# Values of six heads in one token-major product with the forget logits as 6 more columns, values of the other heads two pairs ahead

## What is computed

```python
proj = rms_norm(x, g_pre_mix) @ w_in
mq, mk, mv, fq, fk, fv, f_logit, cvb, cvc, cvh = split(proj)   # 6 x 384, 6, 3 x 256 columns
moba = softmax(causal(mq @ mk.T / 8 + relative_bias)) @ mv     # 6 "local" heads of 64
log_f = log_sigmoid(f_logit + b_f)                             # one logit per head and token
fox = softmax(causal(fq @ fk.T / 8 + cumsum(log_f) differences)) @ fv   # 6 forgetting heads
conv = cvb * causal_conv3(cvc * cvh)
x = x + rms_norm(concat(moba, fox, conv) @ w_out, g_post_mix)
h2 = rms_norm(x, g_pre_ffn)
out = x + rms_norm((silu(h2 @ w_gate) * (h2 @ w_up)) @ w_down, g_post_ffn)
```

## Time and profile before

| what | us |
|---|---|
| median of 3 runs | 581.09 |
| the three runs | 580.45, 581.09, 581.23 |
| the profiled execution's own time | 581.22 |
| its span, first to last instruction | 579.5 |
| TensorE busy in the span | 569.5 |
| values of pair 0 and forget logits on PE | 26.04 to 35.29 |
| the loop's pairs 0 to 4 | 35.29 to about 156 |
| pair 5 | about 156 to 196.8 |

### The profile page before, as it was taken

One profiled execution on the slowest core, in us unless ns is written; L12 is line 12 of the kernel. 1 busy time (PEld: TensorE's weight loads), 2 busy tenths in 40 slices (PEclk: granted clock), 3 DMA queues, 4 the chain that ended last, 5 costly groups with the idle time before them and its releaser, 6 DMA issues.

```text
span 579.5 us, 9678 instructions
## 1 busy us (share of the span) xinstructions
PE 569.5 (98%) x3381; PEld 501.4 (87%) x3381; DVE 472.3 (82%) x788; ACT 322.6 (56%) x540; POOL 113.3 (20%) x128
## 2 busy tenths in 40 slices
PE   6999999999999999999999999999999999999996
PEld 5878888888888888899999999999999988888884
DVE  3868897988849874799888988988898788888797
ACT  6735666666645553656464645455454565547752
POOL 1111011122200010000423233242423013344100
PEclk9999999999999999999999999999999999999999
DMA  7554343333223381312232323132321459999833
GB/s 298 164 152 122 109 110 110 110 96 124 73 74 109 110 312 52 103 44 74 83 136 78 140 72 145 72 113 104 112 105 72 145 167 283 262 212 207 160 145 145
DMA packets 27322, 76.82 MB, mean 133 GB/s; under 512 B 3194, under 2 KB 3194, under 8 KB 27292
## 3 DMA queue, kind: packets, MB, share of 16 engines
q1 hardware_dynamic: 18204, 54.83, 27.0%
q0 software_dynamic: 9088, 21.61, 17.1%
HBM read 69.06 MB, written 4.22 MB: 126 GB/s over the span
## 4 chain that ended last, share of the span: by engine, by line
PE 97%; DMA 1%; ACT 1%; DVE 0%; issue 0%; SPq 0%; DVEq 0%; ACTq 0%
PE bank L1532 11%; PE bank L1534 11%; PE bank L1533 11%; PE bank L1787 8%; PE bank L1786 8%; PE bank L1785 8%; PE bank L1793 6%; PE bank L1851 6%; PE bank L1853 6%; PE bank L1855 6%; PE bank L1796 3%; PE bank L1666 3%; PE bank L1654 2%; PE bank L1578 2%; PE bank L1644 1%; PE bank L1642 1%
## 5 line engine op out<-in xcount | busy, mean ns | idle before, releaser
L1786 PE MATMUL bank<-tok_lo,form_hi 128*128 128x256 f32 x320 | 90.6, 283 | 0.0
L1787 PE MATMUL bank<-tok_hi,form_lo 128*128 128x256 f32 x320 | 90.6, 283 | 0.0
L1785 PE MATMUL bank<-tok_hi,form_hi 128*128 128x256 f32 x320 | 90.5, 283 | 0.0
L1532 PE MATMUL bank<-hn,w_hi 128*128 128x512 f32 (+1 forms) x208 | 79.8, 384 | 0.1
L1534 PE MATMUL bank<-hn,w_lo 128*128 128x512 f32 (+1 forms) x208 | 78.1, 376 | 0.0
L1533 PE MATMUL bank<-hn,w_hi 128*128 128x512 f32 (+1 forms) x208 | 77.8, 374 | 0.0
L1785 PEld LDWEIGHTS bank<-tok_hi,form_hi 128*128 128x128 f32 x320 | 60.9, 190 | 1.9
L1787 PEld LDWEIGHTS bank<-tok_hi,form_lo 128*128 128x128 f32 x320 | 61.1, 191 | 0.0
L1786 PEld LDWEIGHTS bank<-tok_lo,form_hi 128*128 128x128 f32 x320 | 61.0, 191 | 0.0
L1851 PE MATMUL bank<-dw_hi,da_hi 128*128 128x512 f32 x154 | 60.0, 389 | 0.0
L1855 PE MATMUL bank<-dw_hi,da_lo 128*128 128x512 f32 x154 | 59.9, 389 | 0.0
(11 more groups left out here) (201 smaller groups left out, 1394.5 us busy)
## 6 DMA issues: line engine op xcount, KB each, us to landing
raw<-in_w_in_units SPq DMA_DIRECT2D x24, 512.0 KB, 3.4
raw<-in_w_gate_units SPq DMA_DIRECT2D x22, 512.0 KB, 3.3
raw<-in_w_up_units SPq DMA_DIRECT2D x22, 512.0 KB, 4.2
down_x<-in_w_down POOLq DMA_DIRECT2D x15, 512.0 KB, 11.5
down_y<-in_w_down SPq DMA_DIRECT2D x10, 512.0 KB, 11.1
raw<-in_w_out SPq DMA_DIRECT2D x8, 512.0 KB, 3.3
q_lh<-q_hl POOLq DMA_DIRECT2D x12, 256.0 KB, 2.8
down_x<-in_w_down SPq DMA_DIRECT2D x5, 512.0 KB, 4.3
```

The costliest lines, as they stand in the source:

```text
L1532: nc.tensor.matmul(out_ap, sh, mh, start=first, stop=False)
L1785: nc.tensor.matmul(out_ap, sh, mh, start=first and k == 0, stop=False, skip_group_check=True)
L1786: nc.tensor.matmul(out_ap, sh, ml, start=False, stop=False, skip_group_check=True)
L1787: mm = nc.tensor.matmul(out_ap, sl, mh, start=False, stop=k == HK - 1, skip_group_check=True)
```

## The change

**Values of the local heads.** Units 2, 3 and 4 are now the value columns of pairs 0, 1 and 2. They are split, not into slots of the ring, but side by side into two new buffers `wv_hi` and `wv_lo` of 8 x 390 columns; the 6 forget columns stand behind them, as columns 384 to 389. The product is turned round: a tile of 128 tokens is the stationary operand, the 390 columns are the moving one. Four token tiles (groups 2 to 5) take 24 matmuls of 390 columns each, all before the loop. The result is token-major, so these three pairs need neither `vT` nor transposes: ACT and DVE write high and low parts straight into `v_moba`, and DVE copies the 6 logits of each tile to `f_tok`. The first two tiles run high parts first and low parts behind them.

**Forget logits.** Their own group is gone, and the buffer with its memset on POOL. In step 1 of the loop PE transposes `f_tok` in four matmuls into `VTBANK` (`forget_rows`), and `forget_z` follows in step 2 on DVE, the logarithm in step 4 and the running sum in step 6 (before: ahead of the loop, 1 and 5).

**The order of groups.** The value groups of pairs 1 and 2 leave the filler (pair 0's already stood ahead of the loop). The filler has 15 groups in pairs 0 to 4 as before, and 4 in pair 5 instead of 6. The third group of pairs 0 to 2 holds the values of pairs 3 to 5, transposed in step 1 and split in steps 2 and 3 of pairs 1 to 3, two pairs ahead of their use. The third groups of pairs 3 and 4 are the first two groups of the convolution. The splits of units 5 and 6 stand ahead of the loop, behind the evictions of the four value tiles; pair 5 has six splits instead of eight (units 22 to 27).

**Memory.** `v_moba` and a third buffer of `v_fox` lie where `x_sb` lies. So x is loaded a second time for the residual sum: tiles 0 to 2 on SP ahead of unit 20, once the six local heads are done; tile 3 on SP ahead of the third unit of the gate and up weights, once the last head is done. DVE waits for them at the residual sum. `conv_c` and the small rows of the forget logits move as well.

The core of the diff:

```diff
-LO_COL = 32
+V_COLS = MOBA_W + N_FOX
...
+V_TILE = 2
+CONV_GROUPS = (17, 20, 21, 22, 23, 24)
+GROUPS = 25
...
+def v_group(p):
+
+    return 3 * p - 1
+
+
+def kind_of(G):
+
+    if V_TILE <= G < V_TILE + TT:
+        return "v_tile", G - V_TILE, None
+    if G in CONV_GROUPS:
+        return ("conv",) + divmod(CONV_GROUPS.index(G), 3)
+    for p in range(PAIRS):
+        if G - group(p, 0) in (0, 1):
+            return "qk", p, G - group(p, 0)
+    return "v", (G + 1) // 3, None
...
+V_UNITS = (2, 3, 4)
+
+
+def ring_no(u):
+
+    return u if u < V_UNITS[0] else u - len(V_UNITS)
...
+def filler(p):
+
+    first = V_TILE + TT + 3 * p
+    groups = range(first, first + 3) if p < PAIRS - 1 else CONV_GROUPS[2:]
+    return [(G, k) for G in groups for k in range(KT)]
...
+        return [u for at, u in ((0, 3 * p + 7), (1, 3 * p + 8), (5, 3 * p + 9)) if at == s]
+    s = g - 8 * (PAIRS - 1)
+    return [] if s in (2, 3) else [22 + s if s < 2 else 20 + s]
...
-        v_hl = [at("v_hl0", a, [P, TT, 2, P], F32R), at("v_hl1", a + 56 * KB, [P, TT, 2, P], F32R)]
+        v_moba = at("v_moba", 0, [P, MOBA_PAIRS, TT, 2, P], F32R)
+        v_fox = [at(f"v_fox{n}", where, [P, TT, 2, P], F32R) for n, where in enumerate((a, a + 56 * KB, 12 * KB))]
+        wv_hi = at("wv_hi", 48 * KB, [P, KT, V_COLS], F32R)
+        wv_lo = at("wv_lo", 48 * KB + 4 * KT * V_COLS, [P, KT, V_COLS], F32R)
...
+                if u == 20:
+                    sp.wait_ge(pv_done, 2 * MOBA_PAIRS)
+                    for t in range(TT - 1):
+                        load_x(t)
...
+                if j == 2:
+                    sp.wait_ge(pv_done, 2 * PAIRS)
+                    load_x(TT - 1)
...
+                if kind == "v_tile":
+                    nc.scalar.copy(v_moba[:, :, p, :, 0:DH],
+                                   bank[:, PROJ[G % 2], 0:MOBA_W].rearrange("p (b h d) -> p b h d", b=MOBA_PAIRS, h=2)
+                                   ).then_inc(v_hi_done, 1)
+                    return
...
             nc.scalar.preload_act_table_set("natural_log_exp_and_others")
+            for t in range(TT):
+                evac_hi(V_TILE + t)
+            split(5)
+            split(6)
...
+                if kind == "v_tile":
+                    dve.wait_ge(v_hi_done, p + 1)
+                    nc.vector.tensor_tensor(v_moba[:, :, p, :, DH:P],
+                                            src[:, 0:MOBA_W].rearrange("p (b h d) -> p b h d", b=MOBA_PAIRS, h=2),
+                                            v_moba[:, :, p, :, 0:DH], ALU.subtract).then_inc(v_lo_done, 1)
+                    nc.vector.tensor_copy(f_tok[:, p, :], src[:, MOBA_W:V_COLS]).then_inc(proj_read, 1)
...
             evac_lo(group(0, 0))
+            split(4)
             evac_lo(group(0, 1))
-
-            evac_lo(group(0, 2))
-            split(4)
-            forget_z()
+            for t in range(TT):
+                evac_lo(V_TILE + t)
+            split(5)
+            split(6)
 
             conv_lo_at = {6: 0, 9: 1}
...
-                dve.wait_ge(proj_done, F_GROUP + 1)
-                f_bank = PROJ[F_GROUP % 2]
-                nc.vector.tensor_scalar(f_z[:, :], bank[0:N_FOX, f_bank, :], bf_c[:, :], None, ALU.add
+                dve.wait_ge(f_rows_done, 1)
+                nc.vector.tensor_scalar(f_z[:, :], bank[0:N_FOX, VTBANK, :], bf_c[:, :], None, ALU.add
                                         ).then_inc(f_z_part, 1)
                 dve.wait_ge(f_z_part, 1)
-                nc.vector.tensor_tensor(f_z[:, :], bank[LO_COL:LO_COL + N_FOX, f_bank, :], f_z[:, :], ALU.add
-                                        ).then_inc(proj_read, 1)
-                dve.wait_ge(proj_read, F_GROUP + 1)
                 nc.vector.tensor_scalar(f_abs[:, :], f_z[:, :], -1.0, None, ALU.mult).then_inc(f_z_done, 1)
                 dve.wait_ge(f_z_done, 1)
                 nc.vector.tensor_tensor(f_abs[:, :], f_z[:, :], f_abs[:, :], ALU.max).then_inc(f_z_done, 1)
...
                 dve.wait_ge(mix_normed, t + 1)
+                dve.wait_ge(x_in[t], 32)
                 nc.vector.tensor_tensor(x_sb[:, t, :], x_sb[:, t, :], y, ALU.add).then_inc(x1_done, 1)
...
+            def v_pass(t, weight, part, first=False, last=False):
+
+                for k in range(KT):
+                    mm = nc.tensor.matmul(bank[:, PROJ[(V_TILE + t) % 2], 0:V_COLS], part[:, k, P * t:P * (t + 1)],
+                                          weight[:, k, :], start=first and k == 0, stop=last and k == KT - 1)
+                return mm
+
+            pe.wait_ge(hi_done, V_UNITS[-1] + 1)
+            pe.wait_ge(wf_hi_done, 1)
+            for t in range(2):
+                pe.wait_ge(proj_read, t + 1)
+                v_pass(t, wv_hi, hn_hi, first=True)
+                v_pass(t, wv_hi, hn_lo)
+            pe.wait_ge(lo_done, V_UNITS[-1] + 1)
             pe.wait_ge(wf_lo_done, 1)
-            pe.wait_ge(proj_read, F_GROUP - 1)
-            for k in range(KT):
-                for part in (hn_hi, hn_lo):
-                    mm = nc.tensor.matmul(bank[0:LO_COL + N_FOX, PROJ[F_GROUP % 2], :], wf_hl[:, k, :], part[:, k, :],
-                                          start=k == 0 and part is hn_hi, stop=k == KT - 1 and part is hn_lo)
-            mm.then_inc(proj_done, 1)
+            for t in range(2):
+                v_pass(t, wv_lo, hn_hi, last=True).then_inc(proj_done, 1)
+
+            def v_tile(G, t):
+                pe.wait_ge(proj_read, G - 1)
+                tokens_of = slice(P * t, P * (t + 1))
+                for k in range(KT):
+                    mm = product(bank[:, PROJ[G % 2], 0:V_COLS], (hn_hi[:, k, tokens_of], hn_lo[:, k, tokens_of]),
+                                 (wv_hi[:, k, :], wv_lo[:, k, :]), k == 0, k == KT - 1)
+                mm.then_inc(proj_done, 1)
+
+            for t in range(2, TT):
+                v_tile(V_TILE + t, t)
+
+            def forget_rows():
+
+                pe.wait_ge(proj_read, V_TILE + TT)
+                for t in range(TT):
+                    mm = nc.tensor.transpose(bank[0:N_FOX, VTBANK, P * t:P * (t + 1)], f_tok[:, t, :], ident[:, :])
+                mm.then_inc(f_rows_done, 1)
...
-                parts = 3 if p < PAIRS - 1 else 6
-                for m in range(parts):
-                    n = parts * s + m
-                    proj_step(group(p + 1, 0) + n // 8, 3 * (p + 1) + n // 8, n % 8)
-                    if m == parts * 2 // 3:
+                items = filler_at(g)
+                for m, (G, k) in enumerate(items):
+                    proj_step(G, G - 1, k)
+                    if m == len(items) * 2 // 3:
                         if g >= 6 and (g - 6) % 4 == 0:
                             pv((g - 6) // 4)
                         if g >= 2:
                             transpose_step(g - 2)
-                if s == 1:
-                    v_tokens(p)
+                if g == 1:
+                    forget_rows()
+                if MOBA_PAIRS <= p + 2 < PAIRS and s == 1:
+                    v_tokens(p + 2)
```

More of the change, by code:

```diff
@@ L143, in has_hi, with filler_at @@
 def has_hi(G):
-    return G != F_GROUP and G < CONV_GROUP and (G if G < 3 else G - 4) % 3 != 2
+    return kind_of(G)[0] in ("qk", "v_tile")
+def filler(p):
+    first = V_TILE + TT + 3 * p
+    groups = range(first, first + 3) if p < PAIRS - 1 else CONV_GROUPS[2:]
+    return [(G, k) for G in groups for k in range(KT)]
+def filler_at(g):
+    p, s = divmod(g, 8)
+    part = len(filler(p)) // 8
+    return filler(p)[part * s:part * (s + 1)]
 def finished(g):
-    if g < 0:
+    if not 0 <= g < STEPS:
         return []
-    p, s = divmod(g, 8)
-    if p < PAIRS - 1:
-        return [group(p + 1, j) for j in range(3) if (8 * j + 7) // 3 == s]
-    if p == PAIRS - 1:
-        return [CONV_GROUP + m for m in range(6) if (8 * m + 7) // 6 == s]
-    return []
+    return [G for G, k in filler_at(g) if k == KT - 1]
 def splits_at(g):
```

144 lines of the change are left out of this document (78 added, 66 removed).

## The result

| | before | after |
|---|---|---|
| median, us (10 executions each, on the same chip) | 581.04 | 582.85 |
| range of after, us | | 580.66 to 584.08 |
| ratio, with its 95% interval | | 1.003 (1.0018 to 1.0041) |
| the profiled execution, its span, granted clock | 581.22, 579.5, 0.999 | 581.57, 579.9, 0.998 |

One of these ten executions of before took 941.88 us, and one beside the later runs 942.08; the ratios and counts leave both out (without the first the median of before is 580.99). The change makes the kernel slower by 0.3%. I had forecast 579.8 us and a gain, in a range of 578.6 to 581.8. Two things have to be explained: the profiled execution, which is 1.65 us longer than the 579.92 that I had worked out for it, and the median, which lies 1.3 us above the profiled execution where before the two agree.

A forecast was written before the change was run, and what follows sets the result against it. TensorE, busy 569.5 of 579.5 us, was taken to bound the kernel. 581.22 - 4.25 (PE's work) + 2.85 (new wait) + 0.1 (reload) = 579.92, less 0.13 for the median: 579.8 us, range 578.6 to 581.8.

The forecast's parts named there:

- Rival 1: At the loop's start, the standing PE loses its clock, costing another 1.75 us: 581.5 us, no change; chance 0.08.
- a stall of 2.85 us is shorter than both, which speaks against it: Loop's start: the stall is shorter than the 4.2 and 3.17 us without work seen with a low clock.
- My price of it, 1.75: Behind the stall at the loop's start: 3.5 us of work at half pace cost another 1.75 us.
- The term of 16.8 us for the 96 matmuls: Values ahead of the loop: 96 matmuls of 390 columns at 0.175 us each, bounds 16.3 to 21.8 us.
- No wait of PE over 0.5 us elsewhere: Expected profile: apart from one idle time of 2.6 to 2.9 us near 43 us, PE never waits longer than 0.5 us.
- As long as before: After the loop: the chain to the last head's product is unchanged, DVE done after about 5.4 us, PE there after 5.9.
- the new wait: Loop's start, step 0: PE stands about 2.85 us for unit 5's low part, bounds 2.6 to 3.1.
- the work removed in the loop: PE in the loop: values of pairs 1 and 2 -10.9, value transposes -1.3, new logits transposes +0.4 us.
- pair 5: Loop's last pair: PE falls from 39.82 to about 28.5 us, DVE from 28.53 to 24.0 us.
- the reload: Output projection: x tile 3 in flight delays `g_post_mix_b` about 1 us, for 0.1 us of stall, bounds 0 and 2.4.
- rival 2: Values ahead of the loop: 390 columns run as slowly as 512, 21.8 us for the 96, 584.8 us in all; chance 0.08.
- turns the sign at 0.20 us: Part of rival 2: at 0.20 us per 390-column matmul the forecast gain becomes a loss.

The follow-up runs named there:

- after with the reload later: Kernel after with only the reload of tile 3 of x moved behind the sixth weight unit instead of the second: 582.46 us, ratio 1.0021.
- the idle time filled: Kernel after with 11 useless 512-column matmuls put where PE stood, between the first logits and the wait for unit 5: 581.58 us, ratio 1.0004.
- the splits first: Kernel after with the splits of units 5 and 6 ahead of the four value-tile evictions on ACT and DVE: 578.66 us, ratio 0.9955; again 578.96 us.
- the 2.9 and the 1.8 us kernel: Kernel before with PE held behind the loop's first logits by one more wait on a DVE signal, idle 2.9 or 1.8 us: 585.35 and 584.18 us.
- the 3.9 us kernel: Kernel before with PE held at the start of the second projection group until the last normalised tile is there: 586.56 us, ratio 1.0092.

## Why the prediction was wrong

**Rival 1 was the case, and I gave it 0.08.** The step that failed is "a stall of 2.85 us is shorter than both, which speaks against it". I had taken two rows, the clock's fall 4.2 us behind PE's last matmul and the start behind 3.17 us, as the least that it takes. They are each one case: the same fall comes 2.3 to 5.3 us behind PE's end in the fourteen traces, 2.7 in the kernel after. The runs show a lower clock after 1.8, 2.6, 2.9 and 3.9 us in 5 of 8, 13 of 22, 5 of 6 and 5 of 5 executions (the 22 are those of after, and of after with the reload later), and in 5 of 132 without such an idle time (2 of 68 of the kernel before, none of the 12 with the idle time filled, 3 of the 52 with the splits first, where PE waits for up to 1.2 us in the traces' loops). My price of it, 1.75 an execution that has it, was about right: 1.36 in the one trace that shows it (on top of the idle time), 1.4 and 1.6 between the two kinds of executions of the 2.9 and the 1.8 us kernel, 2.1 between those of the kernel after, and 1.3 in its median. The 2.1 is more than a low stretch of 3.4 us can cost, 1.7; what the rest is stays open. Rival 1 alone would have given my 581.5; the rest of the way to 582.85 comes from what follows. The mean clock of one execution is a sign only, as it also holds the end of the span, where PE is done; the rows of the 3.9 us kernel are what shows the fall. In the kernel after itself no traced execution shows it at the stall, and that 1.8 us are enough no trace shows at all: there the cause is inferred from times and mean clocks.

**The pace was mis-sized.** The term of 16.8 us for the 96 matmuls measures 17.36. I had interpolated from two rows of a matmul in a mixed sequence, and my lower bound, 0.17, is one of them. A series of 384 columns takes 0.178.

**One wait was missed.** "No wait of PE over 0.5 us elsewhere" was wrong at 60.91. I had moved the forget work in my sum only for PE (0.4 us), and had looked for room on DVE in pair 5, not in pair 0, where `forget_z` with 1.8 us had come from ahead of the loop into step 2. What it pushes back is DVE's eviction of the queries in its step 4 (59.38), on which PE's next group waits.

**"As long as before" at the last head** was 0.38 us off; DVE's last low part starts at 202.81, not 202.39. It is there too with the splits first (a wait of 0.25), so it doesn't come from the start of the loop. No run takes it apart further.

**Right by their own steps:** the new wait (2.85 forecast, 2.77), the work removed in the loop (-11.8), pair 5 (28.5, and 28.55; DVE 24.0, and 24.62; both windows lack the pair's first 0.95 us, as I had taken 157.00 for its start, which it isn't: 156.05), the reload (0.1, and 0 in the traced execution), and rival 2: 390 columns cost far less than 0.2275. Its "turns the sign at 0.20 us" is wrong: the forecast gain of 1.3 us over 96 matmuls is gone at 0.189, and 0.20 is where the kernel would have been clearly slower. With 0.181 that took half of the gain.

**With the three misses put in** (0.56, 0.85, 0.38, and 0.1 for the start of the values) and less the reload that cost nothing (0.1), the stall's excess (0.08) and the rest (0.07), the sum for the profiled execution is 579.92 + 1.89 - 0.25 = 581.56, where it has 581.57; the clock's 1.3 makes the median of 582.85.

## What to carry to other kernels

When work moves ahead of a loop, look at what stands in the queues of the other engines between it and the loop's first instruction: here two splits behind four evictions turned a gain of 0.45% into a loss of 0.3%, and exchanging them cost nothing. Price an idle time of a busy PE as its length plus the chance of a lost clock, also where it is shorter than the one that the trace shows losing it: how long that takes differs from one execution to the next. And take the cost of an operation from a long series of it, or keep the range open to both sides of the nearest single rows.

## What the runs showed of the hardware

- With PE standing for 1.8 us behind dense work, the mean clock of the execution was lower (0.996 or less) in 5 of 8 executions; with 2.6 us in 13 of 22. With useless matmuls in those 2.6 us it was in none of 12, and they cost nothing there, since PE had to wait anyway (span 579.9 with and without them).
- Behind PE's last matmul the granted clock fell after 2.3 to 5.3 us in fourteen traces (2.7 in the kernel after, 4.2 in the kernel before).
- In one execution PE stood from 34.5 to 38.44 us, the clock fell to 1.2 GHz shortly before 38 and was back at 2.4 GHz shortly after 41; 9 matmuls of 512 columns took 3.48 us there in place of 2.12.
- Matmuls in a long series took 0.178 us with 384 moving columns and 0.181 with 390, where two single ones of 384 columns had taken 0.17; rows 1600 bytes apart in place of 1560 made it 0.179 for 390.
- A weight unit of 512 KB was used 3.8 us behind its issue in one trace and the same unit 7.91 us behind it in another (in the median the units of `w_in` land after 3.4 us, those of the up weights after 4.2), with other transfers of 512 KB issued from 0.4 us later on.
